# Four of the eight K-tile pairs of a feed-forward product by seven products, with weight sums that DMAs accumulate

## The reference, cut to what matters

```python
h = rms_norm(x, ffn_pre_g[l])
gate, up = jnp.split(h @ w_ffn_in[l], 2, axis=-1)      # [256, 2048] @ [2048, 11264]
x = x + rms_norm((jax.nn.silu(gate) * up) @ w_ffn_out[l], ffn_post_g[l])
```

## Time and profile before

| | |
|---|---|
| runs | 2424.85, 2425.55, 2428.86 us; median 2425.55 |
| profiled execution | span 2423.8 us from the first to the last instruction |
| around the span | median less span: 1.75 us; the page gives no other time of this execution |
| PE, DVE, ACT, POOL busy | 2400.0, 1774.4, 1334.3, 36.9 us |
| granted TensorE clock | 0.998 of full speed |

### The profile page before, as it was taken

How to read it: one execution, slowest core, us unless ns; L and a number is a source line. 1 busy time by engine, 2 the same in 40 slices (tenths; PEclk the granted TensorE clock), 3 DMA queues, 4 the chain that set the end, 5 groups by cost and what they waited for, 6 DMA issues and landing times.

```text
span 2423.8 us, 33578 instructions
## 1 busy us (share of the span) xinstructions
PE 2400.0 (99%) x12147; PEld 2002.2 (83%) x12147; DVE 1774.4 (73%) x2434; ACT 1334.3 (55%) x1853; POOL 36.9 (2%) x60
## 2 busy tenths in 40 slices
PE   9999999999999999999999999999999999999998
PEld 7888888897888888878887889998788888887887
DVE  5568888677888888886667436777778888887666
ACT  5665558665555555554445435554655555554444
POOL 1000000000000000000000010000000000000000
PEclk9999999999999999999999999999999999999999
DMA  7765545545556565656566774434565565565655
GB/s 235 242 207 185 164 150 173 168 157 167 189 192 215 190 200 181 199 193 208 188 209 206 218 222 157 144 109 157 160 204 184 194 219 189 193 198 184 215 181 175
DMA packets 233854, 455.83 MB, mean 188 GB/s; under 512 B 16698, under 2 KB 19002, under 8 KB 233232
## 3 DMA queue, kind: packets, MB, share of 16 engines
q1 hardware_dynamic: 227008, 431.49, 55.3%
q0 software_dynamic: 6160, 21.81, 2.6%
q10 hardware_dynamic: 576, 1.05, 0.1%
HBM read 449.04 MB, written 5.24 MB: 187 GB/s over the span
## 4 chain that ended last, share of the span: by engine, by line
PE 92%; DVE 5%; ACT 2%; issue 1%; DMA 1%; DVEq 0%; SPq 0%; ACTq 0%
PE g L1275 14%; PE g L1277 14%; PE g L1276 14%; PE g L348 6%; PE g L350 5%; PE g L349 5%; PE g L1760 4%; PE g L1762 4%; PE g L1761 4%; PE m L1130 2%; PE m L1132 2%; PE m L1131 2%; PE g L1130 2%; PE g L1132 2%; PE g L1131 2%; PE g L2697 1%
## 5 line engine op out<-in xcount | busy, mean ns | idle before, releaser
L336 DVE TENSOR_TENSOR wl<-raw,wh 128x1024 fp32r<-128x1024 f32 (+1 forms) x820 | 987.8, 1219 | 473.6 <-ACT wh L332 457.7
L332 ACT ACTIVATE wh<-raw 128x1024 fp32r<-128x1024 f32 (+1 forms) x819 | 856.3, 1055 | 770.4 <-PE g L1277 247.6
L1275 PE MATMUL g<-wh,act_hi 128*128 128x512 f32 x960 | 374.8, 390 | 0.2 <-DVE shared L1538 0.2
L1277 PE MATMUL g<-wh,act_lo 128*128 128x512 f32 x960 | 373.5, 389 | 0.0
L1276 PE MATMUL g<-wl,act_hi 128*128 128x512 f32 x960 | 373.5, 389 | 0.0
L1275 PE MATMUL g<-wh,ht_hi 128*128 128x512 f32 x544 | 212.0, 390 | 0.0
L1275 PEld LDWEIGHTS g<-wh,act_hi 128*128 128x128 f32 x960 | 180.2, 188 | 38.4 <-issue 0.6
L1276 PE MATMUL g<-wl,ht_hi 128*128 128x512 f32 x544 | 211.8, 389 | 0.0
L1277 PE MATMUL g<-wh,ht_lo 128*128 128x512 f32 x544 | 211.6, 389 | 0.0
L1277 PEld LDWEIGHTS g<-wh,act_lo 128*128 128x128 f32 x960 | 180.2, 188 | 37.7
L1276 PEld LDWEIGHTS g<-wl,act_hi 128*128 128x128 f32 x960 | 180.2, 188 | 37.0
(11 more groups left out here) (517 smaller groups left out, 3889.3 us busy)
## 6 DMA issues: line engine op xcount, KB each, us to landing
raw<-in_w_ffn_in SPq DMA_DIRECT2D x176, 512.0 KB, 4.4
raw<-in_ffn_w_in SPq DMA_DIRECT2D x176, 512.0 KB, 4.5
raw<-in_w_in SPq DMA_DIRECT2D x111, 512.0 KB, 4.6
raw<-in_w_ffn_out SPq DMA_DIRECT2D x88, 512.0 KB, 4.9
raw<-in_ffn_w_out SPq DMA_DIRECT2D x88, 512.0 KB, 4.7
raw<-in_nsa_w_in SPq DMA_DIRECT2D x80, 512.0 KB, 4.3
raw<-in_w_out SPq DMA_DIRECT2D x32, 512.0 KB, 4.5
raw<-in_nsa_w_out SPq DMA_DIRECT2D x32, 512.0 KB, 5.2
```

Of the source, the lines that this page charges most:

```text
L332: nc.scalar.activation(wh[:, j % SLOTS, 0:n], raw[:, j % SLOTS, 0:n], ACT.Copy).then_inc(hi_done, 1)
L336: nc.vector.tensor_tensor(wl[:, j % SLOTS, 0:n], raw[:, j % SLOTS, 0:n], wh[:, j % SLOTS, 0:n].bitcast(F32), ALU.subtract).then_inc(lo_don ...
L1275: nc.tensor.matmul(dst, h, whk, start=(t in starts and k == 0), stop=False)
L1277: ins = nc.tensor.matmul(dst, l, whk, start=False, stop=(last and k == 1))
```

## The change

Four pairs (K-tile pairs 1 to 4) go by sevens. A body becomes 8 plain units and 16 quarters, 24 items. A quarter is named by a letter and the block's number: a (b11, b21; 6 matmuls), b (b22; 3), c (a sum and t4; 6), d (two sums; 6). The weight blocks get tiles of their own, two for each block (`slot_a`, `slot_b`), some of them in x's place: x is kept in DRAM (`pool_keep_x`) while a feed-forward product runs, and is brought back in the output product (`pool_bring_x`). The sums with b12 are made by DMAs that add while they write (`accum_op=ALU.add`), issued by POOL: one into slot_a (b11 becomes b11 + b12) after quarter a is converted, one into slot_b after quarter b is converted and t2 is made. DVE adds two sums of 512 columns to each block (`dve_block_sums`). The first x sum of each block goes into places of `act_hi` and `act_lo` that the sevens don't use.

```diff
-SEVENS = 2
-FF_FIRST, FF_NEXT = 16, 20
+SEVENS, SEVEN_K = 4, 1
+FF_LIST = "G0 a0 b0 a1 a2 b1 G5 a3 b2 G6 b3 c0 d0 U0 c1 c2 d1 c3 G7 d2 d3 U5 U6 U7".split()
+FF_AT = {key: j for j, key in enumerate(FF_LIST)}
+FF_FIRST, FF_NEXT = 16, len(FF_LIST)
+TURN_AT = FF_AT["U6"]
+GATE_END, QUARTERS_END = FF_AT["G7"], FF_AT[f"d{SEVENS - 1}"]
+SUM_AFTER = (6, 7, 10, 13)
+SILU_AT, KEEP_AT, UP_AT, MUL_AT = 1, 12, 1, 13
...
+        def act_quarter(act, name, i, j):
...
+            if q == 0:
+                act.wait_ge(a_in[b], loaded_no(name, i))
+            elif q == 1:
+                act.wait_ge(b_in[b], loaded_no(name, i))
+            elif q == 2:
+                act.wait_ge(ff_step, ff_stepped(name, i, STEPS["t4"][b]))
+            else:
+                act.wait_ge(b12_added[b], added_no(name, i, b, 2))
+            act.wait_ge(unit_used, lo_no(s, i, j) - SLOTS)
+            nc.scalar.activation(quarter_of(wh, j, q), quarter_from(b, q), ACT.Copy).then_inc(hi_done, 1)
...
+        def dve_block_sums(dve, name, i, b):
+
+            a_, b_ = slot_a[b], slot_b[b]
+            dve.wait_ge(b12_added[b], added_no(name, i, b, 1))
+            nc.vector.tensor_tensor(b_[:, 0, :], a_[:, 0, :], b_[:, 1, :], ALU.add).then_inc(ff_step, 1)
+            dve.wait_ge(ff_step, ff_stepped(name, i, STEPS["t2"][b]))
+            nc.vector.tensor_tensor(a_[:, 1, :], b_[:, 0, :], a_[:, 1, :], ALU.add).then_inc(ff_step, 1)
+
+        def pool_block_sums(pool, name):
...
+            with pool.Fori(1, PAIRS) as i:
+                for b in range(SEVENS):
+                    pool.wait_ge(lo_done, lo_no(s, i, FF_AT[f"a{b}"]))
+                    pool.sem_inc(sum_begun, 1)
+                    pool.dma_start(slot_a[b][:, 0, :], b12(i, b), accum_op=ALU.add).then_inc(b12_added[b], 16)
+                for b in range(SEVENS):
+                    pool.wait_ge(lo_done, lo_no(s, i, FF_AT[f"b{b}"]))
+                    pool.wait_ge(ff_step, ff_stepped(name, i, STEPS["t2"][b]))
+                    pool.sem_inc(sum_begun, 1)
+                    pool.dma_start(slot_b[b][:, 1, :], b12(i, b), accum_op=ALU.add).then_inc(b12_added[b], 16)
+
+        def pool_keep_x(pool, name, turn):
+            for n in range(8):
+                pool.wait_ge(lo_evac, bank_no(turn, max(n, 2)) + 1)
+                pool.dma_start(dram_x[:, :, n * HB:(n + 1) * HB], x[:, :, n * HB:(n + 1) * HB]).then_inc(x_moved, 16)
...
+        def pe_quarter(pe, name, i, j):
...
+            pe.wait_ge(lo_done, lo_no(s, i, j))
+            if q == 0:
+                product(0, of_x(0, 0), m[:, 0, :], first, last)
+                ins = product(1, of_x(1, 0), g[:, 0, :], False, False)
+            elif q == 1:
+                ins = product(1, sums_of(3), g[:, 2, :], first, False)
+            elif q == 2:
+                product(0, sums_of(0), m[:, 2, :], first, last)
+                ins = product(1, of_x(1, 1), g[:, 1, :], False, False)
+            else:
+                product(0, sums_of(1), m[:, 3, :], first, last)
+                ins = product(1, sums_of(2), m[:, 1, :], first, last)
+            ins.then_inc(unit_used, 1)
...
             for j in range(FF_FIRST):
                 sp_unit(sp, s["u0"] // SLOTS, j, columns(0, j // 8, j % 8))
...
+            for b in range(2):
+                block_a(1, b)
+                block_b(1, b)
+            for n in range(SLOTS):
+                sp.wait_ge(lo_done, SLOTS + s["u0"] + FF_FIRST - SLOTS + n + 1)
+                unit(1, n)
+            sp.wait_ge(ss_done, SS[turn] + 2)
+            sp.wait_ge(x_moved, x_moved_no(name, 1))
+            for b in range(2, SEVENS):
+                block_a(1, b)
+                block_b(1, b)
 
             def body(i, more):
...
+                for j, key in enumerate(FF_LIST):
...
+                    sp.wait_ge(lo_done, lo_no(s, i, j))
+                    if key[0] == "c":
+                        block_a(i + 1, int(key[1:]))
+                    elif key[0] == "d":
+                        block_b(i + 1, int(key[1:]))
+                    else:
+                        n = FF_UNIT_AT.index(j) + SLOTS
+                        unit(i + n // len(FF_UNIT_AT), n % len(FF_UNIT_AT))
...
-                    if j == 11:
-                        dve_sums_of_x(dve, act_hi, act_lo, 2 * SEVEN_K[0], whole, sums)
...
+                    if j in (9, 12):
+                        dve_sums_of_x(dve, act_hi, act_lo, 2 * SEVEN_K + 4 * (j // 12), whole[j // 12], sums[j // 12])
...
-                    if j == 3:
+                    if j == UP_AT:
                         up_rows(i - 1)
-                    if j == 6:
+                    for b in range(SEVENS):
+                        if j == SUM_AFTER[b]:
+                            dve_block_sums(dve, name, i, b)
+                    if j == MUL_AT:
                         mul(i - 1, 1 - par)
-                    if j == 15:
+                    if j == QUARTERS_END + 2:
                         shared_sums(i)
-                    if j == 18:
-                        dve.wait_ge(unit_used, ff_used(s, i, 13))
+                    if j == FF_NEXT - 1:
+                        dve.wait_ge(unit_used, ff_used(s, i, GATE_END))
```

More of the change, by code:

```diff
@@ new lines, in quarter_of, with quarter_from, dve_quarter @@
+        def quarter_of(buf, j, q):
+            whole_slot = buf[:, j % SLOTS, :].rearrange("p (k n) -> p k n", k=2)
+            return whole_slot[:, 1, :] if q == 1 else whole_slot
+        def quarter_from(b, q):
+            return slot_b[b][:, 1, :] if q == 1 else (slot_a if q % 2 == 0 else slot_b)[b]
+        def dve_quarter(dve, name, i, j):
+            s = gemms[name]
+            q, b = of_block(FF_LIST[j])
+            dve.wait_ge(hi_done, lo_no(s, i, j) - SLOTS)
+            nc.vector.tensor_tensor(quarter_of(wl, j, q), quarter_from(b, q), quarter_of(wh, j, q).bitcast(F32),
+                                    ALU.subtract).then_inc(lo_done, 1)
@@ new lines, in pe_quarter, with product, of_x @@
+        def pe_quarter(pe, name, i, j):
+            s = gemms[name]
+            q, b = of_block(FF_LIST[j])
+            slot = j % SLOTS
+            k0, sums_of, first, last = 2 * (SEVEN_K + b), block_sums(b), b == 0, b == SEVENS - 1
+            def product(half, rows, dst, start, stop):
+                whk, wlk = wh[:, slot, half * NB:(half + 1) * NB], wl[:, slot, half * NB:(half + 1) * NB]
+                nc.tensor.matmul(dst, rows[0], whk, start=start, stop=False)
+                nc.tensor.matmul(dst, rows[0], wlk, start=False, stop=False)
+                return nc.tensor.matmul(dst, rows[1], whk, start=False, stop=stop)
+            def of_x(k, t):
+                return [buf[:, k0 + k, t * P:(t + 1) * P] for buf in (act_hi, act_lo)]
+            pe.wait_ge(lo_done, lo_no(s, i, j))
[11 more added lines that the diff above has]
+            ins.then_inc(unit_used, 1)
@@ L1177, in columns, with unit, block_a @@
                 return s["w"][:, 2 * u:2 * u + 2, bass.ds(i * NB + half * FH, NB)]
+            def unit(i, n):
+                key = FF_LIST[FF_UNIT_AT[n]]
+                sp.sem_inc(raw_full[n % SLOTS], 16 * (FF_NEXT // SLOTS // 2 - 1))
+                sp.dma_start(ff_raw(n).rearrange("p (k n) -> p k n", k=2), columns(i, "GU".index(key[0]), int(key[1:])))\
+                  .then_inc(raw_full[n % SLOTS], 16)
+            def block_a(i, b):
+                sp.dma_start(slot_a[b], columns(i, 0, SEVEN_K + b)).then_inc(a_in[b], 16)
@@ L1179, in sp_ffn_in, with block_b @@
+            def block_b(i, b):
+                sp.dma_start(slot_b[b][:, 1, :], s["w"][:, 2 * (SEVEN_K + b) + 1, bass.ds(i * NB + FH, NB)]).then_inc(b_in[b], 16)
             for j in range(FF_FIRST):
                 sp_unit(sp, s["u0"] // SLOTS, j, columns(0, j // 8, j % 8))
-            def ahead(i, p):
-                sp.dma_start(raw[:, SLOTS, :].rearrange("p (k n) -> p k n", k=2), columns(i, 0, SEVEN_K[p])).then_inc(ahead_in, 16)
-            def body(i, more):
[L1186 to L1198, removed]
@@ L1200, in sp_ffn_in @@
-            ahead(1, 0)
+            turn = {"ff1": "nff", "ff2": "nff2"}[name]
+            for b in range(2):
[9 more added lines that the diff above has]
+                block_b(1, b)
@@ new lines, in body @@
+            def body(i, more):
+                for j, key in enumerate(FF_LIST):
+                    if not more and (key[0] in "abcd" or FF_UNIT_AT.index(j) >= SLOTS):
+                        continue
+                    if key[0] in "ab":
+                        continue
+                    sp.wait_ge(lo_done, lo_no(s, i, j))
[6 more added lines that the diff above has]
+                        unit(i + n // len(FF_UNIT_AT), n % len(FF_UNIT_AT))
@@ L1447, in body @@
[L1447 to L1451, removed]
[L1452 removed]
+                        pe.sem_inc(turn_begun, 1)
+                        pe_ff_turn2(pe)
+                    if key[0] == "G":
```

(15 more changed lines are left out.)

165 lines of the change are left out of this document (118 added, 47 removed).

## The result

The changed kernel takes **2492.6 us** (median of 4 runs, 2491.9 to 2494.9) against 2425.2 us (2424.7 to 2428.9) before: a ratio of 1.0277 [1.0256, 1.0297], 67.4 us slower. The sign was forecast; the size was 18 us, and the time lies 10.6 us above the top of the range.

A forecast was written before the change was run, and what follows sets the result against it. Matmuls on PE were taken to bound the kernel, with DVE close behind. Removed matmuls, waits and other parts summed as -27.2 + 20 x 2.2 + 2 = +18 us, about 2443 us; range 2411 to 2482.

The forecast's parts named there:

- matmuls removed: In the feed-forward input products, 180 matmuls a body for 186: 1.36 us a body, -27.2 us over 20 bodies.
- DVE's load: DVE's work in a body after the change: 38.6 us in 41.4, so DVE goes to 93%.
- L: Time from issue to landing of an addition on POOL's queue, taken as 5.4 us; break-even at 4.5.
- the walk: Item-by-item timing of a body, zero at a1's end on PE: PE loses L - 3.2 = 2.2 us by c1.
- How large L is: Step that set the additions' landing time at 5.4 us, between 4.9 and 5.9, from transfers in the trace.
- At 3.8 it issues a3's addition: POOL's issues in a body: a3's addition at 3.8 us, block 0's second one at 4.55, landing at 4.55 + L.
- nothing, or 0.2 in every second body: Cost of the transposes waiting for shared sums that begin at d3's end, with U5 in between on PE.
- Other parts: Opening, x to DRAM and back, transposes and SP's loads: 2 us in the sum.
- That is a loss of 0.6 us a body: With instant additions, DVE's queue makes c1 ready at 16.17 where PE wants it at 15.64, up to L about 4.
- early landing: Rival: additions land early, only DVE's queue costs, -13 us, 2413 us; decides from L = 4.5 downwards; chance 0.27.
- The additions are slow (L of 6.5 to 7): Rival: d0 and c1 lose 3.3 to 3.8, block 1's sums 0.6 to 0.9 more; 2479 to 2494 us; chance 0.15.
- the forecast's own case: Additions landing in 4.7 to 6.2 us, chance 0.46; about 2443 us, alone 2430 to 2468.

The follow-up runs named there:

- e1: The changed kernel with block 0's second addition issued by POOL ahead of a3's first one: 2427.1 us.
- e6: The changed kernel with U0 before d0, nothing else: 2470.2 us.
- e2: e1 with mul moved from before c1 to behind d3 in DVE's order: 2414.4 us.
- e5: The changed kernel with mul moved behind d3 and POOL's order as in the change: 2482.7 us.
- e8: e7 with U0 before d0 as well: 2411.1 us.
- e3: The changed kernel with the additions made plain copies of the same 256 KB, in the same order: 2422.0 us.
- e4: The changed kernel with additions of 16 columns out of 512, 8 KB each, same order and waits: 2420.9 us.
- e7: e2 with G7 behind d3, so that d2 and d3 come before it: 2413.3 us.

## Why the prediction was right in sign and wrong in size

**Right: matmuls removed, DVE's load.** 120 matmuls fewer; DVE is busy for 386.5 us in ten bodies, where the sum said 38.6 a body.

**Right: the mechanism.** Block 0's second addition is late for ACT at d0, and c1 is late behind block 3's sums and mul. e1 and e6 show the first, e2 and e5 the second. The size at d0 follows too, once its inputs are right: PE is late there by (7.0 + L) - 11.56, with the measured L of 6.1 and an issue 0.6 us later 2.1 us, and the timeline has 1.95, the list of e5 41.6 / 20 = 2.1. At c1 the walk adds 12.35 - 15.64 - 7.0 + 11.56 = 1.3 us in every body; the runs have 0.94, in ten of the twenty (see the clock, below).

**Wrong: the step "How large L is".** It took L = 5.4 from plain transfers and measured 6.1. The lower end came from the only plain transfers of 224 and 256 KB in that queue (4.9 and 5.4 us), outside these stages; plain ones here take 3.0 to 3.5. The price of the adding itself was set at 0.5 us above that end and is 1.4 to 3.1. Two errors, of opposite sign, so that L came out only 0.7 us short is in part luck. Worth 0.7 x 20 = **14 us** by the walk.

**Wrong: the line "At 3.8 it issues a3's addition".** It allowed 0.1 us from the end of a3's conversion on DVE to POOL's issue. The timeline shows 723.07 - 722.36 = 0.71; the earlier trace rows give the length of an issue, and nothing there shows the response of this engine to a semaphore in such a loop. Worth 0.6 x 20 = **12 us** by the walk, in which every us of delay on this path is a us of PE; no run moves this term alone.

**Missing: the clock.** In the kernel before, two stretches of matmuls stand at 0.63 us instead of 0.39, 3.2 us each, both in the output products. In the kernel after there are twelve, ten of them in the stages. From start to start, the 79 matmuls of these ten come 15.7 us later than at 0.2267 each. The prediction had no term for it. But it doesn't come on top in full: the ten bodies with such a stretch are the ten in which PE doesn't wait at c1. The stretch lies between d0 and c1, so it takes the place of that wait of 0.94 us: from d0 to c1 on PE are 5.21 us with the wait (732.35 to 737.56) and 5.72 with the stretch (867.66 to 873.38). Ten such waits would be 9.4 us, so what the clock adds to the walk is 15.7 - 9.4, **some 6 us**. That is an estimate, since no run takes the clock away alone.

The stages lie 42 us over their forecast: 58.6 us more than before, where 20 x 2.2 - 27.2 = 16.8 were forecast. By the distances from start to start in the traces before and after, this divides so:

- The waits at d0 take 47.3 us, those at c1 9.4 and the clock 15.7, together 72.4 where the forecast had 44: 28 of the 42 us. The two wrong steps above explain 26 of them, since with them put right the walk gives 3.5 x 20 = 70. That it comes so close is in part luck: it puts 25 us at c1, where a shorter wait in ten bodies and the clock in the other ten make 25.1.
- The transposes take 15.4 us instead of 12.4, where "nothing, or 0.2 in every second body" stood.
- The last 10 are distances a little over the pace: behind a wait, and at some changes between a quarter and a unit, the second matmul comes 0.34 us after the first instead of 0.23. e8, with hardly a wait, has 4 of these 10; the prediction put 0.1 a body for them.

**Too small: the "Other parts".** +2 us was forecast, 9 came. In the waits, PE's at the end of the openings (`PE g L1455 <- DVE wl L1383`) are 2.3 us; before, the nearest are 1.6 us just inside the stages (`PE g L1130 <- DVE shared L1515`). At the seam to the output product, where its own quarters by seven products begin (`wl L1136`), PE waits 4.8 us in three places, against 0.4 us in two before. In ff1 (3.3 of the 4.8) ACT there waits 2.71 us for a load `raw<-in_w_ffn_out`; in ff2 (1.5) no transfer is late. e8 has 4.4 us of the same waits. Their cause was not tried. The two stretches at half clock in the output products are longer than before (11 and 10 matmuls for 7 and 7, 1.4 us), and about 1 of the 9 us is not placed.

**Too low: the floor.** "That is a loss of 0.6 us a body" for early landing; e3 and e4 have first stages of 424 us, 8 to 9 above the 415.5 that the removed matmuls leave of 429.1, so 0.8 to 0.9. Little of that is the wait at c1 that was named for it (`PE m L1292`: 2.4 us in all of e3, 0.8 in e4); distances of 0.34 us as above are part of it. With 7 us at the ends it makes 2421 to 2422 instead of 2413. With such a floor, the order of the change had at most 4 us to win at any L. That rival held for the mechanism, not for the price.

**The rivals.** "The additions are slow (L of 6.5 to 7)" has the right time, 2479 to 2494, by a wrong road: L was 6.1 to 6.3, and its second part, block 1's sums waiting for a1, did not come. DVE waits for these additions for 0.3 us in the whole run, and the four first additions land in 4.4 us (median of all 80). The measured L of 6.1 to 6.3 is what the forecast's own case (4.7 to 6.2) ends with, for which the sum says 2458 to 2460 us: the range was too narrow because it held L alone; response, clock and restarts had no bounds in it.

## What to carry to other kernels

An engine that issues in program order makes a transfer late through what stands before it in its list: compare the time at which each transfer's source is ready with the time of its issue, and sort the issues by when their results are used. When a wait is covered for one item, look at what queues behind that item on the engine in between (here sums and mul before c1): mul moved alone gave 10 us and U0 before d0 alone 22, of the 81 that e8 gives, while bringing the late landing forward gave 65 by itself. Give a delay on a path that sets the end its own row for every hop, the answer of the issuing engine too, and keep its sum as a bound.

## What the runs showed of the hardware

- A transfer of 256 KB that adds into the on-chip tile lands in 4.3 to 6.3 us (medians by tile; single ones in the kernel after in 4.0 to 9.4), a plain one at the same place in 3.0 to 3.6 (2.8 to 5.0), an adding one of 8 KB in 2.4 to 2.6. POOL's issue takes 0.85 us, up to 1.1 in a pair, against 43.16 / 80 = 0.54 plain.
- Adding takes about 2.1 times the engines' time per byte, an estimate from the queues' shares: the DMA share of a stage rises from 0.69 (e3) to 0.78 (after) and 0.81 (e8), and SP's loads of 512 KB into `raw` land in 4.5 to 4.7 us there (4.4 in e3 and in the earlier trace rows).
- From the end of the DVE instruction that POOL waits for to the start of its issue there are 0.64 to 0.71 us (722.36 to 723.07; again 734.32, the end of the sum that starts at 733.64, to 734.96).
- TensorE's clock fell to 1.2 GHz twelve times in the kernel after, thirteen in e5 and eleven in e6, where PE waits for about 2 us once a body, and twice in the kernel before, in e1 to e4, e7 and e8, where it doesn't. In the stages it fell in 10, 11 and 8 of the 20 bodies, behind such a wait, in e5 once 1.5 us after matmuls had begun again; what decides which is not settled. Where it did, a wait of 1.8 to 3.0 us was followed by 1.2 to 1.7 us of lost time, and the two longest (3.2 and 4.5 us) by 2.4 and 2.0.
